# Block products of the up turns: operands of VectorE in PSUM, one low part moved to VectorE, modulation columns of the down turns a turn later

## The reference, cut to what matters

```python
def _swiglu(h, w13, w2):
    g, u = jnp.split(h @ w13, 2, axis=-1)
    return (jax.nn.silu(g) * u) @ w2

def _sublayer(x, fn, pre_g, post_g, shift, scale, gate, res_w):
    h = _rmsnorm(x, pre_g) * (1.0 + scale[:, None, :]) + shift[:, None, :]
    y = _rmsnorm(fn(h), post_g)
    return x + res_w * (1.0 + gate[:, None, :]) * y
```

## Time and profile before

| what | value |
|---|---|
| median of 3 runs | 3347.24 us (3345.45 to 3353.19) |
| the profiled execution, its own time | 3348.57 us |
| span of the profiled execution, first to last instruction | 3346.7 us |
| TensorE busy | 3061.5 us (91%) |
| VectorE busy | 2288.9 us (68%) |
| ScalarE busy | 1359.0 us (41%) |
| GpSimd busy | 1841.5 us (55%) |
| mean granted TensorE clock | 0.971 of full |

### The profile page before, as it was taken

How to read it: one execution, slowest core, us unless ns; L and a number is a source line. 1 busy time by engine, 2 the same in 40 slices (tenths; PEclk the granted TensorE clock), 3 DMA queues, 4 the chain that set the end, 5 groups by cost and what they waited for, 6 DMA issues and landing times. The chain is left out here.

```text
span 3346.7 us, 57191 instructions
## 1 busy us (share of the span) xinstructions
PE 3061.5 (91%) x22801; PEld 2579.5 (77%) x22801; DVE 2288.9 (68%) x3768; ACT 1359.0 (41%) x2579; POOL 1841.5 (55%) x1293
## 2 busy tenths in 40 slices
PE   5999999899999999789989988999988889999998
PEld 4998876689977998667779966887766667678887
DVE  7998478699955999453589764744677775674443
ACT  3444234444423444124444431324444443435433
POOL 3997342389934998234379943324466772143332
PEclk8999999999999999889999999999999999999999
DMA  6565422146643554333233343312422233222221
GB/s 201 171 189 169 142 83 64 57 140 194 186 138 111 168 166 142 113 90 86 68 104 111 101 134 125 108 57 78 111 56 60 56 95 70 90 71 76 76 73 57
DMA packets 641456, 367.04 MB, mean 110 GB/s; under 512 B 107902, under 2 KB 634132, under 8 KB 640688
## 3 DMA queue, kind: packets, MB, share of 16 engines
q1 hardware_dynamic: 633216, 351.57, 36.0%
q10 hardware_dynamic: 6640, 10.49, 1.0%
q0 software_dynamic: 1344, 1.44, 0.2%
HBM read 334.27 MB, written 24.97 MB: 107 GB/s over the span
## 5 line engine op out<-in xcount | busy, mean ns | idle before, releaser
L270 POOL TENSOR_TENSOR w_lo<-w_raw,w_hi 128x1024 fp32r<-128x1024 f32 (+1 forms) x181 | 425.3, 2351 | 898.4 <-ACT w_hi L262 845.1
L262 ACT ACTIVATE w_hi<-w_raw 128x1024 fp32r<-128x1024 f32 (+1 forms) x172 | 175.0, 1018 | 474.2 <-PE acc L335 348.8
L335 PE MATMUL acc<-h_terms,w_hi 128*128 128x512 f32 x656 | 260.2, 412 | 13.1 <-DVE hid L1376 12.7
L1240 PE MATMUL scaled<-h_terms,h 128*128 128x256 f32 x1856 | 260.5, 283 | 0.0
L335 PE MATMUL acc<-h_terms,w_lo 128*128 128x512 f32 x592 | 239.9, 405 | 0.0
L1240 PEld LDWEIGHTS scaled<-h_terms,h 128*128 128x128 f32 x1856 | 239.4, 192 | 0.0
L335 PE MATMUL acc<-hid,w_hi 128*128 128x512 f32 x528 | 215.6, 408 | 0.0
L335 PE MATMUL lat<-h,w_slots 128*128 128x512 f32 x672 | 199.5, 396 | 4.6 <-ACT plain L3912 4.0
L955 DVE SCALAR_TENSOR_TENSOR ada_part<-ada_raw,c_act,ada_part 128x256 f32<-128x256 f32 x390 | 190.0, 487 | 14.7
L648 DVE TENSOR_TENSOR scaled<-z,x 128x512 f32<-128x512 f32 x36 | 41.0, 1138 | 216.5 <-ACT z L589 216.5
L1107 POOL TENSOR_TENSOR h<-z,h 128x512 fp32r<-128x512 f32 x120 | 179.6, 1510 | 0.0
(11 more groups left out here) (779 smaller groups left out, 9102.9 us busy)
## 6 DMA issues: line engine op xcount, KB each, us to landing
w_raw<-in_ffn_w SPq DMA_DIRECT2D x240, 512.0 KB, 4.2
ada_raw<-in_ada_w SPq DMA_DIRECT2D x88, 1024.0 KB, 5.6
w_raw<-in_od_w_in SPq DMA_DIRECT2D x32, 512.0 KB, 4.1
w_raw<-in_ffn_w SPq DMA_DIRECT2D x32, 384.0 KB, 3.7
w_raw<-in_ev_w_in SPq DMA_DIRECT2D x22, 512.0 KB, 4.0
image<-inverse_wait SPq DMA_DIRECT2D x144, 64.0 KB, 2.1
first_ada<-in_ada_w SPq DMA_DIRECT2D x8, 1024.0 KB, 12.4
w_raw<-in_ab_w_in SPq DMA_DIRECT2D x16, 512.0 KB, 4.1
```

What stands on the lines that cost most here:

```text
L262: act.activation(K.w_hi[:, first % SPLIT, 0:tiles, :], K.raw[:, first % RAW, 0:tiles, :], ACT.Copy).then_inc(K.hi_ready, 1)
L270: pool.tensor_tensor(K.w_lo[:, first % SPLIT, 0:tiles, :], K.raw[:, first % RAW, 0:tiles, :], K.w_hi[:, first % SPLIT, 0:tiles, :].bitcast ...
L335: mm = pe.matmul(out, w[:, slot, k, :], moving(ap, k, tokens), start=first and k == 0 and p == 0, stop=last and k == tiles - 1 and p == le ...
L1240: pe.matmul(out_of[p], hi_of(t, p)[:, k, :], moving[p][:, part, k, :], start=k == 0 and part == HI, stop=False)
```

## The change

- From turn 4 on, ScalarE copies the first half of the u chunk into a PSUM bank (`raise_up`, into `six_bank`), and `sums_first` reads it there. The operand of product 6 is written to the same bank, so `sums_second` has one operand in PSUM. The operation L1338 still has both inputs in SBUF.
- Silu writes to a PSUM bank (`gate_bank`) and `gated` reads it there.
- The low part of product 6 is made by VectorE (`low_six`) and no longer by GpSimd, which makes six in the order 7, 1, 5, 2, 3, 4. In the preparation of turn 3 `low_six(3)` stands ahead of terms 3 and 4 in VectorE's order.
- `sums_second(t+1)` follows `sums_first(t+1)` at once.
- Hidden rows 0 to 3 get their high and low parts during the last up turn. All low parts of hidden rows are VectorE's. The last up turn has no modulation piece.
- In the down turns `ada_pe` for the sum of turn n runs in turn n+1, behind that turn's first chunk, and `ada_write` moves with it. The tables are shifted: 18, 18, 18 and 18 up turns have a piece (before: 19, 19, 19 and 8), and 7, 7, 7 and 6 down turns (before: 7, 8, 8 and 8).
- The down turns use the PSUM banks in a rotation moved by one, the scale of the recurrence is made in down turn 6 and no longer in 7, and `ctx_2` is loaded near the end of the last down half.

```diff
+EARLY = 4
+LO_ORDER = (7, 1, 5, 2, 3, 4)
+LO_PLACE = {p: i + 1 for i, p in enumerate(LO_ORDER)}
+ADA_UP = {0: {t: (t - 3, None) for t in range(3, FB - 1)},
+          2: {t: (t + 22, None) for t in range(3, FB - 1)},
+          3: {**{t: (t + 47, None) for t in range(3, 17)}, **{t: (64 + (t - 17) // 2, (t - 17) % 2) for t in range(17, FB - 1)}},
+          5: {t: (73 + (t - 3) // 2, (t - 3) % 2) for t in range(3, FB - 1)}}
+ADA_DOWN = {0: range(18, 25), 2: range(43, 50), 3: range(66, 73), 5: range(82, 88)}
...
+        hid_hi = lambda j: K.h_first[:, 1, j, :] if j < EARLY else terms[:, hid_place[j - EARLY], :]
...
+        down_bank = lambda n: banks[(n + 1) % 4][:]
+        gate_bank, six_bank = banks[0], banks[1]
...
                 if last:
-                    sp.wait_ge(S.turn_done, count)
+                    sp.wait_ge(K.chunks_done, down.base + 3 * (DB - 1) + 1)
                     sp.dma_start(K.ctx_rows, ...)
...
 # GpSimd
-                    for p in (1, 5, 7, 2, 6, 3, 4):
+                    for p in LO_ORDER:
                         lo(t, p)
...
-                for j in range(8, 13):
-                    pool.wait_ge(S.hid_hi, j + 1)
-                    pool.tensor_tensor(hid[:, j, :], hid_full[:, j, :], hid_hi(j).bitcast(F32), ...)
 # ScalarE
                 def silu(t):
                     act.wait_ge(S.outer, t - PLAIN + 1)
-                    act.activation(hid_full[:, t, :].rearrange("p (a c) -> p a c", a=2), g_rows, ACT.Silu).then_inc(S.sil, 1)
+                    act.wait_ge(S.prod_ready, t)
+                    act.activation(gate_bank[:].rearrange("p (a c) -> p a c", a=2), g_rows, ACT.Silu).then_inc(S.sil, 1)
+
+                def raise_up(t):
+                    chunk_landed(act, t, 1)
+                    if t == PLAIN + 1:
+                        act.wait_ge(S.prod_ready, PLAIN)
+                    else:
+                        act.wait_ge(S.low_six, t - PLAIN)
+                    act.activation(quarter(six_bank), raw_u(t)[:, 0:KH, :], ACT.Copy).then_inc(S.raised, 1)
...
                 for t in turns:
                     if t + 1 < FB:
                         hi(t + 1, 1)
-                        hi(t + 1, 2)
                     else:
                         act.sem_inc(K.hi_ready, 2 * count)
-                        down_hi(0)
-                    copy_first(t)
+                        hidden_hi(0, 2)
                     if t > PLAIN:
                         silu(t - 1)
+                    copy_first(t)
                     if t + 1 < FB:
-                        for p in (7, 5, 6, 3, 4):
+                        for p in (2, 7, 5, 6, 3, 4):
                             hi(t + 1, p)
                     else:
+                        hidden_hi(2, EARLY)
+                        down_hi(0)
                         down_hi(1)
-                hidden_hi(0, 16)
+                    if t + 2 < FB:
+                        raise_up(t + 2)
+                hidden_hi(EARLY, 16)
 # TensorE, down turns
-                    if n < len(ADA_DOWN[index]):
-                        q = ADA_DOWN[index][n]
-                        ada_pe(pe, K, FIRST_ADA + q, K.ada_of(q)[0].vecs, K.ada_acc, S.ada_cols)
+                        if j == 0 and 0 < n <= len(ADA_DOWN[index]):
+                            q = ADA_DOWN[index][n - 1]
+                            ada_pe(pe, K, FIRST_ADA + q, K.ada_of(q)[0].vecs, K.ada_acc, S.ada_cols)
 # VectorE
+                def low_six(t):
+                    dve.wait_ge(S.hi, 7 * (t - PLAIN) + HI_PLACE[6])
+                    dve.tensor_tensor(lo_of(t, 6), sum_full(t, 6), hi_of(t, 6).bitcast(F32), ALU.subtract).then_inc(S.low_six, 1)
...
                 sums_first(PLAIN)
                 sums_second(PLAIN)
+                low_six(PLAIN)
                 term(3, whole[2], b12, b22, ALU.add)
                 term(4, whole[3], b21, whole[1], ALU.subtract)
                 term_lo(1, 1)
...
                     if t + 1 < FB:
                         sums_first(t + 1)
+                        sums_second(t + 1)
                     if t > PLAIN:
                         gated(t - 1)
                     ada_piece(0, 2)
+                    if t + 1 < FB:
+                        low_six(t + 1)
+                    else:
+                        hidden_lo(0, EARLY)
                     combine_left(t)
-                    if t + 1 < FB:
-                        sums_second(t + 1)
...
                 def chunk(n):
+                    if 0 < n <= len(ADA_DOWN[index]):
+                        ada_write(dve, K, S, ada, ADA_DOWN[index][n - 1])
                     if n < len(ADA_DOWN[index]):
                         ...
                         ada_sum(...)
-                        ada_write(dve, K, S, ada, q)
-                    elif index == 0:
+                    if index == 0 and n == DB - 2:
```

More of the change, by code:

```diff
@@ L977, in ffn_phase @@
     with phase(K, *norm_names("post"), *SUB_SEMS, *BORDER_SEMS, "silu_ready", "prod_ready", "ctx_in", "ctx_sums", "ctx_root",
-               "hid_hi", "hid_ready", "hid_pool", "steps", "lam_z", "h_full", "t_added", "t_hi", "t_ready", "sums", "hi", "lo",
-               "first_done", "left_done", "right_done", "turn_done", "copied", "left", "right", "u_second", "outer", "sil", split=False) as S:
+               "hid_hi", "hid_ready", "steps", "lam_z", "h_full", "t_added", "t_hi", "t_ready", "sums", "hi", "lo",
+               "first_done", "left_done", "right_done", "turn_done", "copied", "left", "right", "u_second", "outer", "sil", "raised",
+               "low_six", split=False) as S:
         S.ada_part = S.psum("ada_part", [P, 2, ADA_W])
@@ L996, in ffn_phase @@
         g_rows, u_rows = holes[:, 0, 1:3], holes[:, 1, 2:4]
-        place = [*range(18, 24), 24, 25, 26, 27, 16, 17]
-        hid_place = [*range(20, 28), *range(16, 20), *range(4, 8), *range(12, 16), 28, 29]
-        hid_hi = lambda j: terms[:, hid_place[j], :]
+        hid_place = [*range(20, 28), *range(16, 20), *range(4, 8), 28, 29]
+        hid_hi = lambda j: K.h_first[:, 1, j, :] if j < EARLY else terms[:, hid_place[j - EARLY], :]
         K.sq = terms_full[:, 30:32, :]
@@ L1024, in sum_full @@
         def sum_full(t, p):
+            if p == 6 and t > PLAIN:
+                return quarter(six_bank)
             if p == 3:
@@ L1136, in hi @@
                     elif p == 6:
-                        act.wait_ge(S.sums, 3 * tau + 2)
+                        act.wait_ge(S.sums, 3 * tau + 3)
                     elif p == 3:
@@ L1190, in _ @@
                 plain(2)
+                raise_up(PLAIN + 1)
                 for t in turns:
@@ L1236, in product @@
                 def product(t, p):
-                    pe.wait_ge(S.lo, 7 * (t - PLAIN) + LO_PLACE[p])
+                    if p == 6:
+                        pe.wait_ge(S.low_six, t - PLAIN + 1)
+                    else:
+                        pe.wait_ge(S.lo, 6 * (t - PLAIN) + LO_PLACE[p])
                     for k in range(KH):
@@ L1442, in _ @@
                 gain = K.pcol("norm_post", 48)[:, (layer * NS + sub) * DB:][:, 0:DB]
-                border_dve(dve, K, S, index, gate, gain, 0.5, down_bank, banks[0], chunk, last)
+                border_dve(dve, K, S, index, gate, gain, 0.5, down_bank, banks[1], chunk, last)
 def split_operand_act(act, S, n, src, dst):
```

60 lines of the change are left out of this document (29 added, 31 removed).

## The result

The changed kernel took **3209.49 us** (median of 4 runs, 3208.19 to 3210.57), the kernel before 3349.55 us (median of 4 runs, 3345.45 to 3353.19). The ratio is 0.9582, 95% interval 0.9565 to 0.9599. The profiled execution has a span of 3208.7 us at a mean granted clock of 0.979; before it was 3346.7 us at 0.971, so 138.0 us went.

What follows compares the result with a forecast made beforehand. VectorE was taken to bound the up turns (11.24 us), waits and half clock to lengthen the down halves. Terms 46 + 120 + 5 - 32 = 139 us off 3347.2 gave 3208; whole range 3178 to 3262.

Steps and rivals of the forecast that it cites:

- The up turns are bound by TensorE at 10.52 us: Up turns 5 to 20: VectorE's turn falls from 11.24 to 10.0 us, leaving TensorE's 10.52 as bound; 46 us gained.
- Why L1344 gets short: VectorE's sum in each up turn: 1.52 us falls to 0.68 with an operand in PSUM, 0.84 saved.
- Rival 4: ScalarE's queue blocks at `raise_up` and for `low_six`, delaying GpSimd and TensorE; 3378 at turns of 13.0 us; chance 0.04.
- One of the signs named for a wrong forecast: Up turns: waits for loads on ScalarE would show the forecast wrong; no size given.
- VectorE reading PSUM: Up turns: by the Trainium skill 0.065 us more per operation, 0.26 a turn, VectorE's turn 10.3, still under 10.52.
- The start: Block products at turn 3: `low_six(3)` holds terms 6 us late, half clock costs 2; four phases by 8, 32 lost.
- The down halves: Down turns without waits: 124.3 us in phases 0 and 2, 127.4 in 3, 126.5 in 5; 120 us gained.
- it fits just: First down sum: VectorE ends hidden rows at 12 us, needs up to 8 more; TensorE asks at 20.6.
- (c): Later down sums: VectorE done by 18.5 us for two vectors, TensorE asks at 21.5 instead of 15.5; no wait.
- The tail: Behind the down halves: two waits gone, 7.8 us, against 3 (0 to 6) for the later `ctx_2` load; 5 net.
- From up to down: First down turn: no wait, since rows 0 to 3 are early and VectorE takes 0.6 us a row, TensorE 0.69.
- The total: Whole kernel: 46 + 120 + 5 - 32 = 139 us less, a median of 3208.

Runs made afterwards that it cites:

- the kernel with shared rows: Changed kernel with low parts of hidden rows 0 to 7 on VectorE behind turn 21 and rows 8 to 12 on GpSimd again: 3230.25 us.
- the kernel with both repairs: Changed kernel with `low_six(3)` behind the last `term_lo` and the `ctx_2` load ahead of the fourth weight load: 3173.47 us, ratio 0.948.

## Why the prediction was right, point by point

- **The up turns are bound by TensorE at 10.52 us.** Right, to 0.01 us. VectorE's own need was put at 10.0: a turn of the changed kernel has 0.20 us in brackets and about 0.2 more in small gaps, so some 10.1. The two kernels with one operand back in SBUF agree: 10.1 + 0.85 is 10.95, measured 10.94, and 10.1 + 0.71 for the gate is 10.81, measured 10.80. For the kernel before, "bound by VectorE" holds in phases 0 and 2. In phase 5 VectorE was busy for 153 of 179 us and GpSimd for 174, and TensorE waited for GpSimd's low parts (0.76 us at 1847.41). The gain there was right all the same, since it was reckoned against TensorE's 10.52.
- **Why L1344 gets short.** Here the prediction had the right size for a reason that does not hold. It gave the 0.84 us to the operand in PSUM. The kernel with operand 6 in SBUF has the same 0.69 at that sum: the sum's new place in the turn, ahead of GpSimd's start, is enough. The PSUM operand protects `low_six` instead, which the prediction had at 0.60 without asking what made it so. As both come to the same turn of VectorE, the error didn't show in the time: that is luck.
- **Raw weights copied by ScalarE, waits for loads.** Rival 4 did not come: TensorE is never idle in these turns. One of the signs named for a wrong forecast is there all the same: `raise_up` waits for its load (1.72 us in the turn shown, 3.01 in the next). ScalarE has the time.
- **VectorE reading PSUM.** The surcharge weighed in the prediction is not there: L1361 with one input in PSUM took 1.22 us, L1353 with both in SBUF 1.22; `low_six` 0.68, as any other of its size.
- **The start.** 32 predicted, 30.7 in the timelines, 31.0 by taking it away. 6 us late (5.7 measured: 7.22 less 1.54) and 2 us of half clock (12.24 less 10.48, 1.8). The chain was right too: one waiting instruction ahead of independent ones.
- **The down halves.** 120 predicted, 116.7 measured; each about a microsecond longer than its sum (125.3 for 124.3). In phases 0 and 2 that is the wait of 1.66 us for GpSimd's third weight chunk: the prediction asked only whether the first two were done in time. In phases 3 and 5 it is the first modulation step, which still waits (2.00 and 1.97 us); "it fits just" did not quite. The later steps wait for nothing, as (c) said.
- **The tail.** The load of ctx_2 was put at 3 of at most 6 us; its wait ate all but 0.1 of what phase 5's tail gained, so 3.8. In return phase 0 gave 2.4 that the prediction had not counted. Net 6.3 for 5.
- **From up to down.** The prediction named three causes in one sentence and gave none a price. They measure 5.5 (early rows), 15 (rows not shared with GpSimd), and some 17 for the piece of turn 21, read from the phase that had none. 5.6 us more of this gain are a modulation step less in phase 5.
- **The total.** 139 for 138.0. The terms are off by 0.7 (up turns), 3.3 (down halves), 1.3 (tail), 1.3 (start) and 1.0 (everything else), in both directions. The path was right; that the sum came within 1 us is luck.

## What to carry to other kernels

When two engines block each other over SBUF, ask at what time in the turn each of them works before moving data to PSUM: in this kernel a PSUM operand was worth about 20 us where the other engine was at work, and next to nothing where it was idle. An instruction that waits belongs behind all work that doesn't need it; 0.85 us at the wrong place cost 31 here. And an order that is only good together with a lighter queue should be tried together with it: alone, its turns were slower than those that it replaced (11.7 us for 11.25).

## What the runs showed of the hardware beyond what was expected

- Five waits of 0.3 to 0.7 us, 1.7 us apart, left the granted clock alone (matmuls 0.23 us apart in the kernel with shared rows), 1.54 us of idling ahead of turn 3 did too, nearly (1.18 for 1.12), while 4.39 us brought the next eight matmuls to 2.04. In between, the length of the wait alone doesn't tell: the first modulation step of phases 3 and 5 waited 1.97 to 2.00 us in the changed kernel and in the one with `low_six(3)` last; in the former no matmul behind it was at half pitch, in the latter 8 and 11 were.
- A collision costs the side that comes second, whichever it is: GpSimd's 1.29 us became 1.75 behind VectorE's L1359, and VectorE's 0.69 became 1.82 behind GpSimd. It can cost much more than one instruction of the other side: a low part of 1.84 us took 6.02 beside VectorE's row of ten back-to-back subtractions, seven of which began after it. Elsewhere the two engines took turns; what makes the difference isn't shown.
- Between phases 0 and 2, in code that no edit touches, two nearly equal kernels differed by 2 us. Windows of TensorE at the same point, first the kernel with both repairs, then the one with a wait for each product:

```profile
570.00:590.00 20.00, 17.30 (x90) 12.81 (x89) 10.35 (x13) 9.67 (x14) 5.17 (x2) 1.00 0.18 52
```

```profile
570.00:590.00 20.00, 17.30 (x83) 12.72 (x81) 10.32 (x13) 9.53 (x13) 5.14 (x2) 0.90 0.16 45
```

The clock came back later in one of them. What decides it was not looked into; it sets how small an effect one profile can show here.
